# Hybrid decoder trunk: the pool input's channel tiles first, pooled rows in another buffer, the mix matmuls ahead of the gate tiles

## What is computed

```python
proj = h @ w_in
a_b, a_c, a_u, pool_u, q, k, v, gate_logits = split(proj)
y_conv = a_b * conv3(a_c * a_u)                 # causal, 3 taps per channel
pooled = (cs - cs_lo) / count - pool_u          # trailing means over 2, 4, 8, 16 tokens, 4 groups
y_pool = einsum('bsgc,gcd->bsgd', pooled, pool_w) * pool_scale
y_att  = sliding_window_attention(rotary(q), rotary(k), v, sinks)
branches = [y_conv, y_pool, y_att] @ w_branch   # 512 -> 1024 each
x += (sum(sigmoid(gate_logits) * branches)) @ w_out
```

## Time and profile before

| | us |
|---|---|
| median of 3 runs | 1312.37 (1312.27 to 1313.87) |
| span of the profiled execution, first to last instruction | 1309.2 |
| PE busy | 1256.7 (96%) |
| DVE busy | 936.9 (72%) |
| ACT busy | 753.1 (58%) |
| POOL busy | 86.7 (7%) |

### The profile page before, as it was taken

How to read it: one execution, slowest core, us unless ns; L and a number is a source line. 1 busy time by engine, 2 the same in 40 slices (tenths; PEclk the granted TensorE clock), 3 DMA queues, 4 the chain that set the end, 5 groups by cost and what they waited for, 6 DMA issues and landing times.

```text
span 1309.2 us, 17343 instructions
## 1 busy us (share of the span) xinstructions
PE 1256.7 (96%) x6280; PEld 1051.8 (80%) x6280; DVE 936.9 (72%) x957; ACT 753.1 (58%) x759; POOL 86.7 (7%) x111
## 2 busy tenths in 40 slices
PE   5998999999999998998999999999999999999987
PEld 4996788788888877996788788888888888888865
DVE  5766755644554456666755788989898989898975
ACT  4455543544443455345543677777777777777763
POOL 3042000200000010052000100000000000000010
PEclk9999999999999999998999899999999999999999
DMA  9853455655555554653455399999999999999931
GB/s 307 289 180 116 155 175 179 193 191 184 186 180 191 192 177 145 200 187 112 145 181 173 102 343 321 357 317 359 315 360 313 360 314 362 313 354 332 348 137 49
DMA packets 214818, 307.47 MB, mean 235 GB/s; under 512 B 7840, under 2 KB 169888, under 8 KB 214768
## 3 DMA queue, kind: packets, MB, share of 16 engines
q1 hardware_dynamic: 212480, 302.02, 68.8%
q0 software_dynamic: 1456, 3.99, 1.0%
q10 hardware_dynamic: 832, 0.80, 0.2%
HBM read 305.73 MB, written 1.05 MB: 234 GB/s over the span
## 4 chain that ended last, share of the span: by engine, by line
PE 83%; DVE 5%; POOL 4%; ACT 4%; issue 3%; DMA 1%; DVEq 0%; SPq 0%; POOLq 0%; ACTq 0%
PE ps L1393 34%; PE ps L1407 17%; PE ps L1236 8%; PE ps L1238 8%; PE ps L1237 8%; PE ps L1458 3%; ACT split L545 2%; POOL wsum L509 2%; PE ps L1362 1%; PE ps L1450 1%; DVE split L807 1%; PE ps L1252 1%; DMA raw<-w_in_dram 1%; POOL wsum L514 1%; POOL Y L517 1%
## 5 line engine op out<-in xcount | busy, mean ns | idle before, releaser
L807 DVE TENSOR_TENSOR split<-raw,split 128x2048 fp32r<-128x2048 f32 x286 | 655.2, 2294 | 237.4 <-ACT split L545 229.4
L545 ACT ACTIVATE split<-raw 128x2048 fp32r<-128x2048 f32 x286 | 546.4, 1913 | 184.4 <-PE ps L1238 120.3
L1393 PE MATMUL ps<-split,br 128*128 128x512 f32 x1344 | 329.2, 396 | 0.0
L1393 PEld LDWEIGHTS ps<-split,br 128*128 128x128 f32 x1344 | 249.3, 189 | 53.3 <-DVE split L807 2.4
L1236 PE MATMUL ps<-split,hT 128*128 128x512 f32 (+1 forms) x416 | 164.1, 394 | 8.2 <-DVE split L807 4.6
L1407 PE MATMUL ps<-split,hT 128*128 128x512 f32 x672 | 161.2, 391 | 0.0
L1237 PE MATMUL ps<-split,hT 128*128 128x512 f32 (+1 forms) x416 | 159.8, 384 | 0.0
L1238 PE MATMUL ps<-split,hT 128*128 128x512 f32 (+1 forms) x416 | 159.8, 384 | 0.0
L1407 PEld LDWEIGHTS ps<-split,hT 128*128 128x128 f32 x672 | 125.6, 188 | 25.9
L1393 PE MATMUL ps<-split,hT 128*128 128x512 f32 x576 | 136.5, 392 | 0.5 <-DVE tmp L928 0.5
L1393 PEld LDWEIGHTS ps<-split,hT 128*128 128x128 f32 x576 | 107.1, 188 | 23.2 <-DVE tmp L928 1.2
(11 more groups left out here) (205 smaller groups left out, 1179.8 us busy)
## 6 DMA issues: line engine op xcount, KB each, us to landing
raw<-moe_w_gu_dram SPq DMA_DIRECT2D x224, 512.0 KB
raw<-moe_w_down_dram SPq DMA_DIRECT2D x56, 1024.0 KB
raw<-w_in_dram SPq DMA_DIRECT2D x46, 1024.0 KB
raw<-ffn_w_gu_dram SPq DMA_DIRECT2D x56, 512.0 KB
raw<-ffn_w_down_dram SPq DMA_DIRECT2D x14, 1024.0 KB
raw<-w_branch_dram SPq DMA_DIRECT2D x12, 1024.0 KB
raw<-w_out_dram SPq DMA_DIRECT2D x8, 1024.0 KB
raw<-ple_w_gate_dram SPq DMA_DIRECT2D x8, 1024.0 KB
```

Source lines behind the costliest of these rows:

```text
L545: act.activation(split[:, t % SPLIT, 0, :], raw[:, t % RAW, :], ACT.Copy).then_inc(hi, 1)
L807: dve.tensor_tensor(split[:, t % SPLIT, 1, :], raw[:, t % RAW, :], split[:, t % SPLIT, 0, :].bitcast(F32), ALU.subtract).then_inc(lo, 1)
L1393: ins = pe.matmul(ps[:, bank, :], lhs[:, sl, k0 + k, tokens(b)], slot(t, sr, 512)[:, k, :], start=kind == "a" and k + m == 0, stop=kind == ...
```

## The change

The channel tiles come in the order P, C, U, B. `pooled` moves from the memory of `c_sb` to that of `sg`, so the pooling no longer waits for the convolution to be done with C. The copies of each result move with its tile, two steps earlier for P and two later for C, U and B. The mix matmuls go from behind gate tile 2 to between the last channel tile and gate tile 0, and the instructions that take them out go from step 3 to step 1 of the gate tiles. No arithmetic is added or removed. The core of the diff:

```diff
-MIX, ATT, ATT_OUT = 2, 1, 11
+ATT, ATT_OUT = 1, 11
+CHAN_COLS = (1536, 1792, 512, 768, 1024, 1280, 0, 256)
+CHAN_BANKS = (4, 5, 6, 7, 2, 3, 4, 5)
+POOL_EVAC = 1
...
-        pooled = c_sb
+        pooled = sg[:, :, :].rearrange("p b n -> p (b n)").rearrange("p (c n) -> p c n", c=CH)
...
             def pooling(l):
-                pool.wait_ge(conv_v, 2 * (l + 1))
...
# ACT, channel steps
-                    if j < 2:                      # copy C
+                    if j in (0, 1):                # copy P to upool, chan_out
+                    if j in (2, 3):                # copy C to c_sb, c_copied
-                    if j in (4, 5):                # conv_y -> conv_hi
+                    if j in (6, 7):                # conv_y -> conv_hi
-                    if j in (6, 7):                # copy P
...
# DVE, channel steps
-                    if j in (2, 3):                # U * C
+                    if j in (4, 5):
-                    if j in (4, 5):                # taps, * B, conv_lo
+                    if j in (6, 7):
...
# PE
                     if j in (6, 7):
-                        pe.wait_ge(c_copied, 2 * l + j - 5)
+                        pe.wait_ge(chan_out, 2 * l + j - 5)
                     if j == 5:
-                        pe.wait_ge(conv_y, 2 * l + 1)
+                        pe.wait_ge(c_copied, 2 * (l + 1))
...
+                pe.wait_ge(pooled_ready, CH * (l + 1))
+                pe.wait_ge(small_in, 16 + 96 * (l + 1))
+                pe.wait_ge(conv_v, 2 * (l + 1))
+                for g in range(CH):
+                    ins = pe.matmul(ps[:, 2 + g // 2, ...], poolw_sb[:, g, :], pooled[:, g, :], ...)
+                ins.then_inc(mixed_done, 1)
...
                                 if c == 0 and step == 0:
-                                    pe.wait_ge(chan_out, 2 * l + 1 + b)
+                                    pe.wait_ge(conv_y, 2 * l + 1 + b)
...
-                        if at == MIX:              # the same matmuls, behind gate tile 2
```

More of the change, by code:

```diff
@@ L386, in _ @@
                 fetch(t + 2, [(raw_slot(t + 2, 256), rows(w, 0, KD, OFF_K, 256))])
-                for j, c0 in enumerate((512, 768, 1024, 1280, 0, 256, OFF_POOL, OFF_POOL + 256)):
+                for j, c0 in enumerate(CHAN_COLS):
                     u = t + T_CHAN + j
@@ L671, in _ @@
                     split_hi(t0 + T_CHAN + j + 2)
-                    if j < 2:
+                    if j in (0, 1):
                         act.wait_ge(tile_used, t0 + T_CHAN + j + 1)
-                        act.activation(c_sb[:, 2 * j:2 * j + 2, :],
+                        act.activation(upool[:, 2 * j:2 * j + 2, 16:],
+                                       ps[:, 4 + j, :].rearrange("p (c n) -> p c n", c=2), ACT.Copy
+                                       ).then_inc(chan_out, 1)
+                    if j in (2, 3):
+                        act.wait_ge(tile_used, t0 + T_CHAN + j + 1)
+                        act.activation(c_sb[:, 2 * (j - 2):2 * (j - 2) + 2, :],
                                        ps[:, 4 + j, :].rearrange("p (c n) -> p c n", c=2), ACT.Copy
                                        ).then_inc(c_copied, 1)
-                    if j in (4, 5):
-                        act.wait_ge(conv_y, 2 * l + j - 3)
-                        act.activation(brv[:, 0, 2 * (j - 4):2 * (j - 4) + 2, :], ctmp, ACT.Copy
-                                       ).then_inc(conv_hi, 1)
                     if j == 5:
@@ L687, in _ @@
                     if j in (6, 7):
[L688 to L691, removed]
+                        act.wait_ge(conv_y, 2 * l + j - 5)
+                        act.activation(brv[:, 0, 2 * (j - 6):2 * (j - 6) + 2, :], ctmp, ACT.Copy
+                                       ).then_inc(conv_hi, 1)
                 for c in range(6):
@@ L697, in _ @@
                             softmax_exp(l, at - ATT - 2)
-                        if at == MIX + 1:
+                        if at == POOL_EVAC:
                             act.wait_ge(mixed_done, l + 1)
@@ L880, in mask_scores @@
                 dve.wait_ge(s_done, 6 * l + u + 1)
+                if u == 0:
+                    dve.wait_ge(conv_lo, 2 * (l + 1))
                 if u > 2:
@@ L1044, in _ @@
                     cs = slice(2 * (j % 2), 2 * (j % 2) + 2)
-                    if j in (2, 3):
+                    if j in (4, 5):
                         dve.wait_ge(tile_used, t0 + T_CHAN + j + 1)
-                        dve.wait_ge(c_copied, 2 * l + j - 1)
-                        dve.tensor_tensor(vpad[:, cs, 2:], ps[:, 4 + j, :].rearrange(
+                        dve.wait_ge(c_copied, 2 * l + j - 3)
+                        dve.tensor_tensor(vpad[:, cs, 2:], ps[:, CHAN_BANKS[j], :].rearrange(
                             "p (c n) -> p c n", c=2), c_sb[:, cs, :], ALU.mult).then_inc(conv_v, 1)
-                    if j in (4, 5):
+                    if j in (6, 7):
                         dve.wait_ge(small_in, 16 + 96 * (l + 1))
-                        dve.wait_ge(conv_v, 2 * l + j - 3)
+                        dve.wait_ge(conv_v, 2 * l + j - 5)
                         for c in range(2):
-                            ch = 2 * (j - 4) + c
+                            ch = 2 * (j - 6) + c
                             chain(dve.tensor_scalar(cacc[:, c, :], vpad[:, ch, 0:SEQ], convw_sb[:, ch, 0:1],
@@ L1062, in _ @@
                         dve.wait_ge(tile_used, t0 + T_CHAN + j + 1)
-                        dve.tensor_tensor(ctmp, ps[:, j - 2, :].rearrange("p (c n) -> p c n", c=2), cacc,
-                                          ALU.mult).then_inc(conv_y, 1)
-                        dve.wait_ge(conv_hi, 2 * l + j - 3)
+                        dve.tensor_tensor(ctmp, ps[:, CHAN_BANKS[j], :].rearrange("p (c n) -> p c n", c=2),
+                                          cacc, ALU.mult).then_inc(conv_y, 1)
+                        dve.wait_ge(conv_hi, 2 * l + j - 5)
                         dve.tensor_tensor(brv[:, 1, cs, :], ctmp, brv[:, 0, cs, :].bitcast(F32),
@@ L1534, in _ @@
                     pe.wait_ge(pT_lo, 1)
-                for j, bank in enumerate((4, 5, 6, 7, 2, 3, 4, 5)):
+                for j, bank in enumerate(CHAN_BANKS):
                     t = t0 + T_CHAN + j
@@ L1565, in _ @@
                         ins.then_inc(qk_turned, 1)
+                pe.wait_ge(pooled_ready, CH * (l + 1))
+                pe.wait_ge(small_in, 16 + 96 * (l + 1))
+                pe.wait_ge(conv_v, 2 * (l + 1))
+                for g in range(CH):
+                    ins = pe.matmul(ps[:, 2 + g // 2, g % 2 * SEQ:(g % 2 + 1) * SEQ],
+                                    poolw_sb[:, g, :], pooled[:, g, :], start=True, stop=True)
+                ins.then_inc(mixed_done, 1)
                 for c in range(6):
@@ L1598, in _ @@
                         ins.then_inc(tile_used, 1)
-                        if at == MIX:
[L1600 to L1606, removed]
                         for stage, late in ((att_values, 4), (att_turn, 3), (att_scores, 0)):
```

## The result

The changed kernel takes 1302.09 us (median of 4 runs, 1299.70 to 1303.72) against 1313.12 us before (median of 4, 1312.27 to 1314.19). The ratio is 0.9911, with a 95% interval of 0.9900 to 0.9923: 10 to 13 us faster. The forecast was 1301.0, with a range of 1298 to 1305.

What follows compares the result with a forecast made beforehand. PE bounds the kernel, busy 1256.7 of 1309.2 us, so only its waits or slow work can be won. 17.25 - 2 x 2.95 = 11.35 us of gain gave 1301.0 us, range 1298 to 1305.

Steps and rivals of the forecast that it cites:

- first to third scores: PE's distance from scores of unit 0 to unit 2: 13.5 us against 21.59 and 22.75, removing 17.25 in both layers.
- The 3.2 us: Time around the profiled span, from 1309.2 us to the median of 1312.37, taken to stay.
- The pooling: POOL's pooling starts near 44 us, ends near 71, before the mix matmuls at 84.83, so their wait goes.
- The mix: Mix matmuls ahead of gate tile 0, at the full clock: 1.7 us a layer on PE's path.
- Bank 5: In gate tile 0's second half PE waits for DVE to read the second B result: about 1.25 us.
- The walk: Convolution's chain from measured distances: DVE splits at 76.45 and 84.70, second product with B ending at 90.45.
- The mask: PE's second scores wait 0.8 us for DVE's `masked`, which comes 7.1 us after the first scores.
- The moved reads: ACT's four mix-result reads need 1.57 us, idle time there is 1.56: cost 0, at most 0.3 a layer.
- The rule that spoke against it: DVE and POOL exclude each other: channel tile 2's split late, PE losing 0.2 us in layer 0, giving 1301.2.
- that rival: Clock falls in the new waits, or POOL holds DVE up in convolution and splits: 1305.7 us, 11%.

Runs made afterwards that it cites:

- e1: The changed kernel measured again, nothing altered: 1303.16 us (6 runs), ratio 0.9926.
- e4: The kernel before, in its old order, with the pooling cut to one instruction for each group (pooled rows not the model's): 1297.62 us, ratio 0.9890.
- e2: The changed kernel with the mix matmuls back behind gate tile 2 and pooled rows in other memory: 1306.47 us, ratio 0.9954.
- e8: The kernel before with only the mix matmuls moved ahead of gate tile 0, channel tiles in the old order: 1338.58 us (one run).
- e3: The changed kernel with DVE's taps ahead of the splits in the last two channel steps, finally the product with B too: 1299.71 us, ratio 0.9898.
- e5: The changed kernel with the pooling cut to one instruction for each group: 1303.13 us, ratio 0.9920.
- e6: The changed kernel with DVE's mask (and the scaling at step 4) ahead of the splits at gate steps 2 to 4: 1301.79 us, ratio 0.9908.
- e7: The changed kernel with the DVE reorderings of e3 and e6 together: 1296.82 us, ratio 0.9879.

## Why the prediction was right

The forecast was 11.35 us of gain. Its own terms, summed over both layers: first to third scores gave 21.59 - 13.46 + 22.75 - 13.41 = 17.47 us (17.25 forecast). What was paid ahead of them is the mix to the first scores, 99.00 - 85.05 = 13.95 and 583.99 - 570.02 = 13.97, less the 10.92 of two gate tiles: 6.1 us (5.9 forecast). That leaves 11.4 us. In this stretch the mechanism and the sizes are right, in e1 as in the first profile. The PE row with the mix of layer 1:

```profile
570.02 1.89 PE L1553 MATMUL ps<-sg,poolw_sb 128*128 128x256 f32 x8
```

That the total came out so close is in part luck. The forecast let all that follows the third scores shift as a whole, and the two profiles do not: PE is ahead by 117.34 - 112.46 = 4.88 us at the third scores of layer 0, by 573.91 - 570.02 = 3.89 where the channel tiles of layer 1 end, by 10.18 at the third scores of layer 1 and by 7.2 at the end. The medians gave 11.0 us the first time and 9.3 in e1. The 3.2 us that the forecast put around the span were 1.7, and the rest was that the profiled execution was faster than the median; this leaves the forecast as it is, since it amounts to taking 11.35 from the median.

*The pooling.* Right: the wait is gone, and the pooling ends at 71.62, forecast near 71. e4 shows that the pooling's length was the cause of the wait and of the low clock behind it, e2 that the new channel order alone takes both away at that place, and e8 that the new place of the mix alone does not.

*The mix* takes 86.58 - 85.05 = 1.53 us to the next matmul. What it costs on PE's path is read in e3, where no wait follows it: 12.62 - 10.92 = 1.70 us, and 1.7 was forecast.

*Bank 5.* The walk gave an end of the second product with B at 90.45, and it ended at 89.96 + 0.69 = 90.65, with the whole trace 0.2 us later than the one before. The wait is 1.05 in the profile and costs 13.95 - 12.62 = 1.33 us on PE's path; 1.25 was forecast. (The forecast's terms as written give 90.45 - 89.26 = 1.19. The 0.06 us to 1.25 is the time from the end of the releasing instruction to PE's start, as from 107.52 to 107.58 in its own rows, which it doesn't name.) e3 shows the cause.

```profile
76.64 2.29 DVE L788 TENSOR_TENSOR split<-raw,split 128x2048 fp32r<-128x2048 f32 x1 [1.51 <-ACT split L526]
...
84.90 2.29 DVE L788 TENSOR_TENSOR split<-raw,split 128x2048 fp32r<-128x2048 f32 x1 [1.11 <-ACT split L526]
...
89.96 0.69 DVE L1046 TENSOR_TENSOR tmp<-ps,M 128x512 f32<-128x512 f32 x1
```

The splits of the walk, put at 76.45 and 84.70, stand at 76.64 and 84.90.

*The mask.* The wait is 0.44 us, forecast 0.8. `masked` ends 105.75 + 0.15 - 99.00 = 6.90 us after the first scores, forecast 7.1: without POOL beside it DVE was faster by more than the two instructions that I corrected. The second scores start 6.96 us after the first, forecast 7.16. The rest of the difference in the wait, here and at bank 5, is that the profile counts it from the modelled end of the last matmul, and I from the time when the next could start. DVE's row:

```profile
105.75 0.15 DVE L875 TENSOR_TENSOR esk<-sinks_sb,mx 128x4 f32<-128x4 f32 x1
```

*The moved reads* fit into ACT's gap: the second sigmoid ends where it did relative to its tile, and the split behind it starts 0.70 us after the first scores (99.70 - 99.00), no later than before.

*The rule that spoke against it.* The split of channel tile 2 was not delayed: two splits took 4.50 us from 45.90 on, and it was POOL that waited: 2.26 us at 45.98 and 2.67 us at 48.32, for instructions that take 0.19 us (at 55.61) and 0.74 us (at 55.88) without it. Later splits beside POOL were longer by up to 0.36 us (2.65 at 57.57), with slack to spare. That one of the two blocks the other as a whole, as the Trainium skill has it ("SBUF — State Buffer", "Who interferes with whom"), agrees with these rows. In e5 nothing of it reaches PE: the waits and distances are the same without the pooling.

```profile
45.90 4.50 DVE L788 TENSOR_TENSOR split<-raw,split 128x2048 fp32r<-128x2048 f32 x2
...
57.57 2.65 DVE L788 TENSOR_TENSOR split<-raw,split 128x2048 fp32r<-128x2048 f32 x1 [3.47 <-ACT split L526]
```

*The rivals.* The clock did not fall in the new waits. But my argument against that rival, that it had stood at 1.00 after more than 2 us of idle time, was weaker than I took it for: in e2 the clock was still at 1.00 during a wait of 2.75 us, and low right behind it. With a wait for B of 2.75 us instead of 1.05 the forecast would have missed 1.6 us a layer, which is most of what this rival stands for.

*What is open.* Why the low clock at the routing lasted longer in both profiles of the changed kernel than in that of the kernel before is not settled, and it is more than a difference between two executions. All ten kept profiles have PE reach that place (the matmuls with `sel`, L1619 in the changed kernel) 127.1 to 127.3 us after the third scores of layer 1. Over the same 19 us the granted clock was 0.76 before, 0.73 in e2 and e4, 0.64 in e3 and e8, and 0.56 to 0.57 in the changed kernel, e1, e5, e6 and e7. The windows of e2 and e8:

```profile
727.67:746.67 19.00, 16.56 (x72) 14.46 (x71) 13.52 (x32) 12.23 (x12) 1.22 (x2) 0.73 0.21 61
```

```profile
757.63:776.63 19.00, 16.77 (x71) 14.72 (x70) 12.82 (x32) 11.93 (x11) 1.22 (x2) 0.64 0.18 56
```

So all seven kernels with the mix ahead of the gate tiles are lower than the three with it behind gate tile 2, and since e8 has the old channel order and e2 the new one, it does not go with the channel order. In time the line is less sharp: from the `sel` matmuls to the matmuls at L1433 (L1450 before) it is 1266.85 - 734.87 = 531.98 us before and 1259.56 - 724.65 = 534.91 in the changed kernel, 533.4 to 533.6 in e2, e3, e4 and e8, and 535.0 to 535.1 in e1, e5, e6 and e7. With one profile of each kernel this is a pattern and no proof that the place of the mix causes it, and how it could is not shown.

## What to carry to other kernels

When a side engine's latency bounds a stage, look first at where its input is made: eight tiles in another order gave it the time it needed, with no instruction added. Then walk the work that was moved back with the measured distances between its instructions, queue by queue; here that gave the new wait to 0.2 us, and said what to reorder next. A consumer's short instruction behind a long one that nobody needs soon is the cheapest thing to mend: exchanging the two on DVE was worth 2.7 us in one place (e3) and 1.6 in the other (e6), by the distances over both layers.

## What was not expected of the hardware

Behind a wait of 2.75 us TensorE's granted clock was at 0.5 for about 3 us (e2, both layers, 1.6 us of cost each). Behind waits of 1.05 us in the same gate tile it was not (the changed kernel, e1, e5 and e6: the granted clock is 1.00 from 84 to 130 us in all four profiles, and in each of the eight places it is 13.95 to 14.02 us from the mix to the first scores). So at this place a wait of 2.75 instead of 1.05 us costs 1.7 + 1.6 = 3.3 us a layer and not 1.7. What stands ahead of the wait is not quite the same in both, since the mix comes there only in the changed order.
